# A recurrent layer's triangle inversion with its turns made whole transposes, and the last norm cut in two

## The reference, cut to what matters

```python
def step(state, inp):                       # rwkv7_mixer, one token, per head, state 64 x 64
    r_t, w_t, k_t, v_t, kk_t, a_t = inp
    sa = einsum('bhij,bhj->bhi', state, -kk_t)
    state = (state * w_t[:, :, None, :] + sa[..., None] * (kk_t * a_t)[:, :, None, :]
             + v_t[..., None] * k_t[:, :, None, :])
    return state, einsum('bhij,bhj->bhi', state, r_t)
```

## Time and profile before

| | us |
|---|---|
| median of 3 runs | 3926.53 (3926.44 to 3931.94) |
| the profiled execution | 3928.47 |
| its span, first to last instruction | 3926.7 |
| PE busy | 3636.5 (93%) |
| VectorE busy | 2545.4 (65%) |
| ScalarE busy | 1596.3 (41%) |
| GpSimd busy | 689.1 (18%) |

### The profile page before, as it was taken

One profiled execution on the slowest core, in us unless ns is written; L12 is line 12 of the kernel. 1 busy time (PEld: TensorE's weight loads), 2 busy tenths in 40 slices (PEclk: granted clock), 3 DMA queues, 4 the chain that ended last, 5 costly groups with the idle time before them and its releaser, 6 DMA issues. The chain is left out here.

```text
span 3926.7 us, 66142 instructions
## 1 busy us (share of the span) xinstructions
PE 3636.5 (93%) x25476; PEld 3148.2 (80%) x25476; DVE 2545.4 (65%) x5090; ACT 1596.3 (41%) x3573; POOL 689.1 (18%) x698
## 2 busy tenths in 40 slices
PE   8999999999999999999899999888889999988887
PEld 6888766788788876898778998777777799987776
DVE  4888547677755567655456776776563577776764
ACT  4222537322332335543335444444432454444443
POOL 0100002000000002000000244444300003444442
PEclk9999999999999999999999999999999999999999
DMA  6555211355434430554135799999942268999998
GB/s 254 202 189 187 81 54 44 110 185 183 156 113 140 140 103 33 194 183 165 62 110 192 307 420 420 421 421 421 418 152 88 97 227 360 420 420 421 420 421 331
DMA packets 135194, 909.48 MB, mean 232 GB/s; under 512 B 14807, under 2 KB 16087, under 8 KB 34016
## 3 DMA queue, kind: packets, MB, share of 16 engines
q0 software_dynamic: 93952, 615.72, 38.9%
q1 hardware_dynamic: 40928, 289.53, 20.5%
HBM read 904.11 MB, written 5.28 MB: 232 GB/s over the span
## 5 line engine op out<-in xcount | busy, mean ns | idle before, releaser
L2916 PE MATMUL ps<-arena 128*128 128x128 f32 x6560 | 829.1, 282 | 138.8 <-ACT arena L2981 137.8
L2916 PEld LDWEIGHTS ps<-arena 128*128 128x128 f32 x6560 | 786.0, 195 | 189.0 <-ACT arena L2981 182.4
L3123 DVE CUSTOM_DVE_ANT_0 arena<-arena 128x1024 f32<-128x1024 f32 x410 | 502.6, 1226 | 283.2 <-DMA arena<-peer_uv,arena 279.5
L3097 POOL DMA_INDIRECT arena<-peer_uv,arena x410 | 446.1, 1088 | 1360.7 <-DVEq L3058 792.4
L714 DVE TENSOR_TENSOR w_lo<-wt,w_hi 128x1024 fp32r<-128x1024 f32 x389 | 476.6, 1225 | 309.9 <-ACT w_hi L696 283.2
L749 PE MATMUL ps<-h_hi,w_hi 128*128 128x512 f32 (+1 forms) x1744 | 636.7, 367 | 6.7 <-ACT h_hi L942 3.5
L696 ACT ACTIVATE w_hi<-wt 128x1024 fp32r<-128x1024 f32 x389 | 408.8, 1061 | 575.8 <-PE ps L749 546.0
L749 PE MATMUL ps<-h_hi,w_lo 128*128 128x512 f32 (+1 forms) x1744 | 627.6, 362 | 0.0
L749 PE MATMUL ps<-h_lo,w_hi 128*128 128x512 f32 (+1 forms) x1744 | 586.5, 361 | 0.5 <-DVE h_lo L962 0.5
L749 PEld LDWEIGHTS ps<-h_hi,w_hi 128*128 128x128 f32 x1744 | 331.2, 190 | 64.8 <-issue 11.1
L749 PEld LDWEIGHTS ps<-h_hi,w_lo 128*128 128x128 f32 x1744 | 331.2, 190 | 51.7 <-issue 1.9
(11 more groups left out here) (363 smaller groups left out, 5323.9 us busy)
## 6 DMA issues: line engine op xcount, KB each, us to landing
wt<-wstream SPq DMA_DIRECT2D x245, 1024.0 KB, 4.9
ada_t<-adastream POOLq DMA_DIRECT2D x128, 512.0 KB, 3.6
arena<-wstream SPq DMA_DIRECT2D x18, 1024.0 KB, 7.8
arena<-adafirst SPq DMA_DIRECT2D x8, 1024.0 KB, 15.0
arena<-peer_uv,arena POOLq DMA_INDIRECT x410, 19.6
arena<-bias_by_query POOLq DMA_DIRECT2D x2, 3072.0 KB, 14.9
bias_by_query<-bias_by_distance POOLq DMA_DIRECT2D x1, 4096.0 KB, 16.8
xT<-tokens SPq DMA_DIRECT2D x2, 1024.0 KB, 7.3
```

What stands on the lines that cost most here:

```text
L2916: ins = pe.matmul(y_banks(t)[m // 4][:, (m % 4) * P:(m % 4 + 1) * P], row[:, D + m * P:D + (m + 1) * P], diag[n % DIAGS], start=s == 0 and ...
L3097: pool.indirect_dma_start(out=rows[at % GB], out_offset=None, in_=peer_uv, in_offset=bass.IndirectOffsetOnAxis(ap=experts[:, t, s:s + 1], ...
L3123: dve.tensor_tensor_reduce(u, u, ztok[:, t], 1.0, 0.0, ALU.mult, ALU.add, hbuf[:, t, s:s + 1]).then_inc(dot_ready.sem, 1)
```

## The change

1. The triangles of level 0 and of XT stay as they were, but the triangle LT for all later levels is made by a second gram (`gram_turned`) with chunk and head swapped: the head's parity u % 2 in the partition half and (u // 2, c) in the columns. So bt and at_ are multiplied twice.
2. The turn is four whole transposes a tile (both g). A transpose of 128 x 128 swaps chunk and head pair as well, so X comes out in the swapped layout.
3. The first products (`first`) read partition half q (head parity) and write half r (chunk), over all four quadrants, into two banks; one ACT instruction of 512 columns copies both banks to Y in the old layout. X is copied by one instruction of 512 columns a tile too. The level's signals are counted by tile, and a dummy claim keeps the pair of banks together (`odd_at`).
4. On DVE nearly all waits for its own instruction are dropped; a bank is set free by the instruction that read it. The four sums of a level come first, then the masks of the grams, then the level masks. PE waits for `D_.free` ahead of a turn. kt and rt are computed later.
5. The grams "ka", "br", "kr" are made behind the second products, in all five levels (LATER_AT), and kt's transposes in level 1. The products with LAK are made ahead of those with atok for both tiles.
6. The root of tile 0 is taken by ACT ahead of group (1, 5) of the expert stage, and DVE normalizes tile 0 in eight steps of 128 columns behind the first eight dots of group (1, 6): for the next layer into hT, at the end into ztok (ztok's tile 0 is no longer needed). Behind the stage the root and norm cover tile 1 alone. The output's layout in memory is (P, 2, D), and it is stored in two halves, the first when the last row has landed.

```diff
-            dve_norm(dve, LAT, "ln1", l * DC)
+            dve_norm(dve, slice(P if l else 0, LAT), "ln1", l * DC)
...
+        LATER_AT = {1: [("ka", 0), ("ka", 1)], 2: [("br", 0)], 3: [("br", 1)], 4: [("kr", 0)], 5: [("kr", 1)]}
...
+            def gram_turned(a, b, t):
+                pe.wait_ge(D_.free, D_.given_back(2))
+                banks = [D_.claim() for _ in range(2)]
+                for u in range(4):
+                    for c in range(2):
+                        x = slice(t * P + c * CH, t * P + (c + 1) * CH)
+                        at = (u // 2 * 2 + c) * CH
+                        for g, r in enumerate(ROWS):
+                            mm(banks[g][ROWS[u % 2], at:at + CH], a[r, u, x], b[r, u, x],
+                               inc=D_.full if u == 3 and c else None)
...
-            def turn(t, g):
-                pe.wait_ge(mix_ready.sem, mix_ready.due(pe))
-                by_rows(A_, XT[t][g], lambda u, c, r: ident[r, c * CH:(c + 1) * CH])
+            def turn(t):
+                pe.wait_ge(A_.free, A_.given_back())
+                bank = A_.claim()
+                for g in range(2):
+                    for p in range(2):
+                        ins = pe.transpose(bank[:, (2 * g + p) * P:(2 * g + p + 1) * P],
+                                           XT[t][g][:, 2 * p:2 * p + 2].rearrange("p u j -> p (u j)"), ident)
+                ins.then_inc(A_.full, 1)
+            def first(t):
+                pe.wait_ge(A_.free, A_.given_back(2))
+                banks = [A_.claim() for _ in range(2)]
+                for g in range(2):
+                    pe.wait_ge(level_ready.sem, level_ready.due(pe))
+                    for p in range(2):
+                        for s, q in enumerate(ROWS):
+                            for c, r in enumerate(ROWS):
+                                mm(banks[s][r, (2 * g + p) * CH:(2 * g + p + 1) * CH], LTL[t][g][q, 2 * p + c, :],
+                                   X[t][g][q, 2 * p + c, :], inc=A_.full if g and p and c else None)
...
             for level in range(1, LEVELS):
-                for i, (t, g) in enumerate(CHAINS):
-                    pe.wait_ge(level_ready.sem, level_ready.due(pe))
+                for t in range(2):
                     pe.wait_ge(turned_ready.sem, turned_ready.due(pe))
-                    by_rows(A_, LTL[t][g], lambda u, c, r: X[t][g][r, u, :])
-                    if coming and i % 2:
-                        ...
-                        gram(*grams[name], of)
-                for t, g in CHAINS:
+                    first(t)
+                added = {}
+                for t in range(2):
                     pe.wait_ge(act_ready.sem, act_ready.due(pe))
-                    by_rows(D_, Y[t][g], lambda u, c, r: XT[t][g][r, u, :])
+                    for g in range(2):
+                        by_rows(D_, Y[t][g], lambda u, c, r: XT[t][g][r, u, :])
+                        added[t] = D_.claimed
+                for name, of in LATER_AT[level]:
+                    if (name, of) in (("ka", 0), ("br", 0)):
+                        pe.wait_ge(late_ready.sem, late_ready.due(pe))
+                    if (name, of) == ("ka", 0):
+                        tokens(kt)
+                    gram(*grams[name], of)
                 if level < LEVELS - 1:
-                    for c in CHAINS:
-                        turn(*c)
+                    for t in range(2):
+                        pe.wait_ge(D_.free, added[t])
+                        turn(t)
...
+            for two in (CHAINS[:2], CHAINS[2:]):
+                marks = [step.mark(masked_by(XT[t][g], const("level", 0, CH))) for t, g in two]
+                for i, (t, g) in enumerate(two):
+                    step.reached(marks[i])
+                    dve.sem_inc(D_.free, 1)
+                    marks[i] = step.mark(dve.tensor_tensor(XT[t][g], XT[t][g], four(const("same")), ALU.add))
+                for i, (t, g) in enumerate(two):
+                    step.reached(marks[i])
+                    dve.sem_inc(mix_ready.sem, 1)
+                    marks[i] = step.mark(masked(LT[t][g], "before"))
+                for i, (t, g) in enumerate(two):
+                    step.reached(marks[i])
+                    dve.sem_inc(D_.free, 1)
+                    level_of(t, g, 1).then_inc(level_ready.sem, 1)
+            dve.tensor_tensor(kt, kmod, pinv, ALU.mult).then_inc(late_ready.sem, 1)
             for level in range(1, LEVELS):
-                for _ in range(2):
-                    ...
                 for t, g in CHAINS:
-                    added(XT[t][g])
-                    dve.sem_inc(mix_ready.sem, 1)
-                    ...
+                    added(t, g)
+                for name, t in LATER_AT[level]:
+                    for g in range(2):
+                        ...
+                        ins.then_inc(D_.free, 1)
+                if level < LEVELS - 1:
+                    for t, g in CHAINS:
+                        level_of(t, g, level + 1).then_inc(level_ready.sem, 1)
...
+        def act_peer_root(act, step, t):
+            seg = slice(t * P, (t + 1) * P)
+            act.wait_ge(total_ready.sem, total_ready.due(act))
+            act_rsqrt(act, step, rstd[:, seg], total[:, seg], 1.0 / D, eps)
+            act.sem_inc(rstd_ready.sem, 1)
...
+                if (t, h) == (1, 5):
+                    act_peer_root(act, step, 0)
...
+                    if (t, h) == (1, 6) and s % PEER_K < DC:
+                        dve_first_tile(dve, l, s % PEER_K)
...
+            sp.wait_ge(row_full[(2 * N_SLOTS - 1) % GB], 16 * ((2 * N_SLOTS - 1) // GB + 1))
+            sp.wait_ge(first_out, DC)
+            sp.dma_start(out[:, 0, :], ztok[:, 0, :]).then_inc(out_done.sem, 16)
             sp.wait_ge(phase_done, 4 * max(phases.values()))
-            sp.dma_start(out, hT[:, :, 0:LAT]).then_inc(out_done.sem, 16)
+            sp.dma_start(out[:, 1, :], ztok[:, 1, :]).then_inc(out_done.sem, 16)
```

More of the change, by code:

```diff
@@ new lines, in pe_rwkv_core @@
+            if odd_at[l]:
+                pe.wait_ge(A_.free, A_.given_back())
+                A_.claim()
+                pe.sem_inc(A_.full, 1)
+            grams = dict(ka=(kt, at_), br=(bt, rt), kr=(kt, rt))
+            for t in range(2):
+                gram(bt, at_, t)
+                gram_turned(bt, at_, t)
+            for src in (zv, at_, bt):
+                tokens(src)
+            for t in range(2):
+                pe.wait_ge(mix_ready.sem, mix_ready.due(pe, 2))
+                turn(t)
@@ L1953, in four, with rows_of @@
                 return ap.unsqueeze(1).to_broadcast([P, 4, CH])
-            def masked(dst, mask):
-                dve.wait_ge(D_.full, D_.filled())
-                bank = D_.take()
-                step(dve.tensor_tensor(dst, bank[:, 0:4 * CH].rearrange("p (u j) -> p u j", j=CH), four(const(mask)),
-                                       ALU.mult))
-                dve.sem_inc(D_.free, 1)
+            def rows_of(bank):
+                return bank[:, 0:4 * CH].rearrange("p (u j) -> p u j", j=CH)
@@ L1962, in masked_wide, with masked_by @@
+            def masked_by(dst, mask):
+                dve.wait_ge(D_.full, D_.filled())
+                return dve.tensor_tensor(dst, rows_of(D_.take()), four(mask), ALU.mult)
+            def masked(dst, mask):
+                return masked_by(dst, const(mask))
             def masked_wide(dst, mask):
                 dve.wait_ge(D_.full, D_.filled())
-                bank = D_.take()
                 wide = [P, 4, 2, CH]
-                step(dve.tensor_tensor(
+                return dve.tensor_tensor(
@@ L1967, in masked_wide @@
                     dst.rearrange("p u (c j) -> p u c j", j=CH),
[L1968 to L1972 removed]
+                    rows_of(D_.take()).unsqueeze(2).to_broadcast(wide),
+                    const(mask).rearrange("p (c j) -> p c j", j=CH).unsqueeze(1).to_broadcast(wide), ALU.mult)
@@ L1973, in added @@
+            def added(t, g):
                 dve.wait_ge(D_.full, D_.filled())
-                bank = D_.take()
-                step(dve.tensor_tensor(dst, dst, bank[:, 0:4 * CH].rearrange("p (u j) -> p u j", j=CH), ALU.add))
-                dve.sem_inc(D_.free, 1)
+                dve.tensor_tensor(XT[t][g], XT[t][g], rows_of(D_.take()), ALU.add).then_inc(D_.free, 1)
             def level_of(t, g, level):
-                step(dve.tensor_tensor(LTL[t][g], LT[t][g], four(const("level", level, CH)), ALU.mult))
@@ L1981, in dve_rwkv_core @@
-            coming = list(LATER)
-            step(dve.tensor_tensor(kt, kmod, pinv, ALU.mult))
-            dve.sem_inc(late_ready.sem, 1)
-            for t in range(2):
-                for g in range(2):
-                    masked(LT[t][g], "before")
-                    level_of(t, g, 0)
-                    step(dve.tensor_tensor(XT[t][g], LTL[t][g], four(const("same")), ALU.add))
-                    dve.sem_inc(mix_ready.sem, 1)
-                    level_of(t, g, 1)
```

(1 more changed line is left out.)

118 lines of the change are left out of this document (69 added, 49 removed).

## The result

| us | before | after | forecast |
|---|---|---|---|
| median | 3926.54 | 3900.12 (3899.24 to 3902.04) | 3906.5 |
| ratio, with its 95% interval | | 0.993 (0.9913 to 0.9947) | 0.995 |
| span of the profiled execution | 3926.7 | 3898.9 | |
| first core, second core | 57.4, 57.4 | 46.4, 45.9 | 48.8 each |
| entry of layer 2: start of the squares' sum to PE's projection | 3.92 | 3.56 | 0.35 less |

Of the 27.8 us between the two spans, 22.5 lie in the cores, 3.5 at the end and 0.36 at the entry of the second layer.

The account below looks back on a forecast made before the run. DMA bounds the expert stages; elsewhere engine-to-engine chains do, in the core VectorE's turn at each level's end. Cores 17.2, end 2.5 and layer-2 entry 0.35 sum to 20.0 us saved: 3906.5 against 3926.53, range 3900 to 3917.

Parts of the forecast that it names:

- a level: Core, triangle inversion: levels after the first start 6.75 us apart, the level mask being late behind the gram's masks.
- the fall of the clock charged to each core: TensorE's clock in the core: one fall of 1.5 us added to each, making 10.1 saved into 8.6.
- the store: Kernel's end: output stored in two halves, 512 KB landing in 3.6 us against 1024 KB in 4.8, 1.2 less.
- VectorE's own waits: Core: dropping them saves 0.23 us a step; rival that this gives nothing: 4.5 a core, 3915.5, chance 0.10.
- the crossing: First products over four quadrants: taken as free; without four-way overlap 0.55 us a level, 5.5 over ten levels.
- the switches: PE changing between whole transposes and quarter-array products, two a level: taken as free; at 0.27 each, 5.4 us worse.
- the stretch ahead of the levels: Core from its first gram to level 1: four grams, 24 transposes, turn and copy; level 1 starts at 1879.3 against 1880.05.
- the root in the stream: Tile 0's root on ScalarE inside the expert stage, 3.3 us or 4.6 with a third load: costs nothing; stalled, 2 a layer.
- second rival: Core: the crossing or the switches cost 5.4 us each or both, time 3912 to 3917, chance 0.16.
- the third: Rival: clock stays low in the core, PE's pieces double, 11 us slower in all, 3937.6, chance 0.05.
- the fourth: Rival: another chain replaces VectorE's in the core, periods stay near 9 us, time 3921, chance 0.06.
- (a): PE's unit costs in the core: 0.017 us a record over four quadrants, 0.036 on the diagonal two, 0.2 until the result.

Follow-up runs that it names:

- e5: Changed kernel with VectorE's waits for itself put back after each sum, gram mask and level mask of the levels; 3909.42 us in one run.
- e3: Changed kernel with VectorE's level masks ahead of the masks of that level's grams; 3892.68 us in one run.
- e6: Changed kernel with first products ordered so that two consecutive ones fall on the same quadrant before the next; 3899.48 us in one run.
- e4: Changed kernel with level masks first, turns ahead of the gram on PE, and copies of kt's transposes moved from level 1 to 2; 3893.80 us, ratio 0.9915.
- e9: Changed kernel with two needless 512-column products on PE, into a free bank, just ahead of the core; 3897.26 us in one run.
- e1: Kernel before with the core's half of the change alone (items 1 to 5); 3905.31 us, ratio 0.9945.
- e8: Changed kernel with the second half of the output kept in hT and stored in 512 B pieces instead of 4 KB; 3899.85 us in one run.
- e2: Kernel before with the ends' half of the change alone (item 6: root, norm, store); 3922.60 us, ratio 0.999.
- e10: Kernel before with one needless 128x128 product on PE behind each turn of the levels; cores 58.9 and 58.1 us against 57.4.
- e11: Changed kernel with turns ahead of the grams, level masks ahead of gram masks, and two needless products ahead of the core; 3889.81 us, ratio 0.9906.

## Why the prediction was right or wrong

**What failed.** The mechanism held; the sizes did not. Three terms of the sum were too cautious: a level (6.75 us, measured 5.95 to 6.18), the fall of the clock charged to each core (1.5, for one in the levels, where none came; the one ahead of them cost 0.4 and 0.9), and the store (1.2 saved, measured 2.2). One effect stood at nothing, PE's idle gaps, and worked the other way. The four follow.

**Right.** That VectorE's own waits cost 0.23 a step and were on the path (e5). That in a level the late one is the level mask behind the gram's masks (e3). That neither the crossing (e6) nor the switches (rows of e4) cost anything to be seen. That the stretch ahead of the levels and level 1 gain little more than the steps say: 8.8 and 7.26 against 9.3 and 7.65. The root's 0.2 and the norm's 1.1 at the end, the 0.35 at the entry (3.92 to 3.56), and the root in the stream: three loads in 4.7 us, with DMA at 1.01. From the end of the second core to the last row's products it is 929.30 us before and 929.32 after. The second rival's crossing and switches cost nothing, the third (clock low in the levels) is refuted by the 1.00 of the levels, the fourth by their periods.

**Mis-sized: the level, by the pace of diagonal products in (a) and by a mask.** The forecast read thirty-two records in 1.15 and divided by 32, 0.036 each, and then added 0.2 until the last result; but the 1.15 hold that tail already: (1.15 - 0.2) / 31 = 0.031. After, 96 records, 64 of them diagonal, take 2.55; with 0.2 of tail and 32 grams at 0.017, the diagonal ones come to (2.55 - 0.2 - 0.54) / 64 = 0.028. So the seconds take about 1.9 and not 2.3, the gram's masks start at 4.18 instead of 4.7, and a level would be 6.2. Of the two level masks that the forecast then waited for, only the first is needed: PE began at 1890.85, 0.14 behind it, which is another 0.3 and gives the 5.95. The level of 6.18 began only behind ScalarE's copy of the second tile, through at 1896.99. Over levels 2 to 4 that is 2.0 us in the first core and 1.8 in the second. The two turned grams were priced alike, at 1.1; without the fall one takes 0.69 (e9), with it 1.0 to 1.2, so there the error hid behind another.

**Mis-sized: the charge for the clock, 1.5 a core.** The size was right for a fall that meets the levels: before's cost 1.5, and the one in the last stretch of e1's first core made 172 records take 5.88 us, where e8's took 4.60 at full clock:

```profile
1905.13 4.60 PE L526 MATMUL ps<-arena 64*64 64x64 f32 x172 [1.32 <-issue]
```

What failed is that one would come there. After's levels had none, in either core. A fall came in the stretch ahead of them, at a price of 0.4 and 0.9 (e9). It is seen ahead of the old core too, in e2 and e10, so it isn't the middle one moved; why it comes, and why the middle one stayed away, is open, and e1 shows that the new core isn't safe from one. That stretch stayed below its full-clock forecast even so, by 0.5 and 0.2, since its turned grams were priced too high. In e4 a fall twice as long hit 24 transposes that stand on the path and the levels began at 10.3 us rather than 8.8: the price depends on its length and on what it meets, and where it falls wasn't to be seen in the trace of before.

**Not foreseen: gaps of "issue" on PE.** The last stretch took 12.2 and 11.1 instead of 10.1. In the kernel without any gap (e3) it took 10.4 and 10.1. It is the one term that worked against the change: the last stretches took back 3.1 of what the others brought beyond the forecast, of which 2.8 are gaps.

The cores' sum: forecast 48.8 each, measured 46.4 and 45.9, 5.2 us in all. That is 3.0 of the clock's charge, 3.8 of levels 2 to 4 and 1.5 of the stretches ahead of level 2 (16.0 and 16.3 against 16.9), less 3.1 of the last stretches.

**Mis-sized: the store.** The forecast took 4.8 against 3.6 of another queue, 1.2. From issue to the end of the span it was 2.2: 1.5 for the volume and 0.7 because the halves in ztok are stored in 4 KB pieces (e8). The forecast looked at KB alone and left the shape of the transfer out, though it had noted that the half comes out of ztok.

The cores' 5.2 and the end's 1.0 (3.5 against 2.5) are 6.2 of the 6.4 us between forecast and result.

**Still not settled.** What the "issue" gaps are. After's first core, e1, e6 and e8 have one at the same place, 20 records into the second products of the last level, and e3, e4, e9 and e11 don't:

```profile
1902.58 0.80 PE L526 MATMUL ps<-arena 64*64 64x64 f32 x20 [0.20 <-ACTq L2005]
1904.72 5.88 PE L526 MATMUL ps<-arena 64*64 64x64 f32 x172 [1.34 <-issue]
```

This is e1, with 1.34 us. The record points at the supply of instructions. They come in packets of 16 KB on a queue of their own, 198 in after for PE's 50,088 recorded products and weight loads, about 253 a packet; between after's first two gaps lie 127 products, between the last two of its second core 128. The DMA view of after in slices of 0.2 us from 1903.00 shows two packets, at 1903.8 and 1907.4, and the gaps end at 1906.30 and 1910.14:

```profile
DMA  0000200000000000000000400000000000000000
```

All 43 gaps in the cores of these kernels end 2.2 to 2.9 us behind the start of such a packet. From level 1 on packets are 3.7 to 6.8 us apart before and 3.4 to 5.8 after, so a core that issues faster has less in hand. That fits a PE that runs out of instructions; no kernel here changed the supply, so it stays unproven.

## What to carry to other kernels

When a pace is taken from n records, take the tail off first: a batch's length holds (n - 1) intervals and one latency, and the error grows with each batch priced. VectorE's waits for its own last write were worth 0.23 us each here, since its chain was the late one, and what is queued between that chain and its consumer (wide masks ahead of level masks) cost another 0.4 to 0.65 a level; look for the independent step that stands in front of the dependent one. Count only what the consumer really waits for: the first of two signals may be enough. Before charging a clock fall, ask which instructions it can meet, and keep both that price and none in the range.

## What the runs showed of the hardware

- Float32 64 x 64 products over all four quadrants cost about 0.017 us a record, in by_rows order on the diagonal two 0.028 to 0.031. In one order among the quadrants 64 records took 1.38 to 1.40 us, in another 1.42 to 1.47.
- A store of 512 KB landed in 2.6 us from 4 KB pieces and in 3.2 from 512 B pieces; 1024 KB in 1 KB pieces took 4.8 before.
- A root taken as logarithm and exponential between other functions cost three table loads of 1.28 us each, not two.
- The granted clock fell in the first 9 us of after's cores (0.81) and in the middle of before's, and in both places with the same old core in e2. Four recorded products of 512 columns just ahead of the core went with 1.00 (e9, e11). A fall in the levels cost 1.3 to 1.5 us.
- PE stood idle 0.2 to 1.3 us in batches of short products with nothing to wait for, up to 2.9 us in a core of 49, and each gap ended 2.2 to 2.9 us behind the start of a packet of instructions.
